# Latent attention's rotary part in one product: queries repacked two heads to a tile by moves within SBUF, and unread products in TensorE's pauses before two norms

## What is computed

```python
def rms_norm(x, g):
    y = xf * lax.rsqrt(jnp.mean(xf * xf, axis=-1, keepdims=True) + EPS)
    return y * g
...
hn = rms_norm(h, g_mix_pre); proj = hn @ w_in              # first block opens
...
h = h + rms_norm(merged @ w_out, g_mix_post)
hn = rms_norm(h, g_ffn_pre); f_gate, f_up = split(hn @ w_ffn_in)
...
q = (rms_norm_2(c_q, q_norm_g) @ w_uq)                     # 8 heads of 128 + 64
q_nope, q_rope = split(q, [128]); q_rope = rotary(q_rope)
k_nope, v = split(rms_norm_2(c_kv, kv_norm_g) @ w_ukv)
k_rope = rotary(k_rope)                                    # 64, shared by all heads
s = q_nope . k_nope + q_rope . k_rope                      # per head, 256 x 256
p = softmax(s * scale); o = p @ v
```

## Time and profile before

| | us |
|---|---|
| median of 3 executions | 2379.6 (2379.14 to 2380.88) |
| the profiled execution | 2379.67 |
| its span, first to last instruction | 2377.9 |
| TensorE busy | 2141.1 (90%) |
| VectorE busy | 1195.1 (50%) |
| ScalarE busy | 685.8 (29%) |
| GpSimd busy | 627.0 (26%) |

### The profile page before, as it was taken

One profiled execution on the slowest core, in us unless ns is written; L12 is line 12 of the kernel. 1 busy time (PEld: TensorE's weight loads), 2 busy tenths in 40 slices (PEclk: granted clock), 3 DMA queues, 4 the chain that ended last, 5 costly groups with the idle time before them and its releaser, 6 DMA issues.

```text
span 2377.9 us, 23241 instructions
## 1 busy us (share of the span) xinstructions
PE 2141.1 (90%) x7018; PEld 1291.6 (54%) x7018; DVE 1195.1 (50%) x2884; ACT 685.8 (29%) x1487; POOL 627.0 (26%) x545
## 2 busy tenths in 40 slices
PE   7999998999999999999897788889989998878786
PEld 6868886888885855444442222248644443322222
DVE  2982112000141035666666666633466666666664
ACT  1112101110110122343444343433243434343442
POOL 0210000000000001444454444410044555444442
PEclk9999998999999999999999999999999999999999
DMA  5443342444354325999999999983399999999997
GB/s 216 146 159 137 139 157 90 150 150 145 138 214 144 139 106 220 421 422 421 421 422 421 422 422 422 422 353 120 142 422 421 422 422 421 422 421 422 422 422 319
DMA packets 97560, 702.55 MB, mean 295 GB/s; under 512 B 10960, under 2 KB 11216, under 8 KB 12240
## 3 DMA queue, kind: packets, MB, share of 16 engines
q0 software_dynamic: 73728, 536.90, 54.3%
q1 hardware_dynamic: 21024, 149.96, 17.4%
q10 hardware_dynamic: 2736, 14.74, 1.6%
HBM read 700.51 MB, written 1.05 MB: 295 GB/s over the span
## 4 chain that ended last, share of the span: by engine, by line
PE 56%; DMA 30%; ACT 5%; issue 5%; DVE 3%; POOL 1%; DVEq 0%; POOLq 0%; ACTq 0%
DMA arena<-uv,expert_index 30%; PE acc L428 30%; PE aux L765 12%; PE acc L456 4%; PE aux L619 3%; PE acc L687 2%; PE acc L775 1%; ACT arena L1186 1%; ACT arena L1189 1%; ACT L1186 1%; PE aux L498 1%; ACT L1178 1%; DVE arena L1743 1%; POOL arena L963 1%; DVE arena L1380 1%
## 5 line engine op out<-in xcount | busy, mean ns | idle before, releaser
L765 PE MATMUL aux<-arena 128*128 128x512 f32 x2048 | 1007.7, 621 | 187.1 <-ACT arena L1189 182.3
L963 POOL DMA_INDIRECT arena<-uv,expert_index x512 | 601.4, 1175 | 1079.4 <-PE aux L765 606.6
L1743 DVE SCALAR_TENSOR_TENSOR arena<-arena 128x1024 f32<-128x1024 f32 x512 | 633.2, 1237 | 427.3 <-DMA arena<-uv,expert_index 426.5
L765 PEld LDWEIGHTS aux<-arena 128*128 128x128 f32 x2048 | 366.9, 193 | 728.2 <-ACT arena L1189 439.3
L428 PE MATMUL acc<-x,w_ring 128*128 128x256 f32 x2352 | 518.5, 384 | 14.6 <-DVE x L1344 9.3
L428 PEld LDWEIGHTS acc<-x,w_ring 128*128 128x128 f32 x2352 | 452.6, 193 | 79.9 <-issue 8.7
L1186 ACT ACTIVATE arena<-ident,dots 128x128 f32<-128x128 f32 x512 | 205.3, 401 | 704.6 <-DVE arena L1743 703.0
L428 PE MATMUL acc<-arena,w_ring 128*128 128x256 f32 x1032 | 225.0, 379 | 3.7 <-DVE arena L1440 1.6
L428 PEld LDWEIGHTS acc<-arena,w_ring 128*128 128x128 f32 x1032 | 195.7, 190 | 31.7 <-issue 2.6
L1189 ACT ACTIVATE arena<-arena,gate 128x128 f32<-128x128 f32 x512 | 205.4, 401 | 17.0
L949 POOL IOTA arena<- 128x512 int32 x1 | 0.6, 558 | 542.7 <-DVEq L1492 542.7
(11 more groups left out here) (250 smaller groups left out, 1169.9 us busy)
## 6 DMA issues: line engine op xcount, KB each, us to landing
w_ring<-stream SPq DMA_DIRECT2D x141, 1024.0 KB, 4.8
arena<-uv,expert_index POOLq DMA_INDIRECT x512, 14.9
first_query_weights<-first_heads ACTq DMA_DIRECT2D x4, 1024.0 KB, 14.3
row_vectors<-rows ACTq DMA_DIRECT2D x3, 1024.0 KB, 12.4
scratch<-keys ACTq DMA_DIRECT2D x2, 1024.0 KB, 6.2
x<-first_heads ACTq DMA_DIRECT2D x2, 1024.0 KB, 4.7
x<-x_cm SPq DMA_DIRECT2D x1, 1024.0 KB, 5.5
arena<-rows ACTq DMA_DIRECT2D x1, 1024.0 KB, 4.5
```

What stands on the lines that cost most here:

```text
L765: last = nc.tensor.matmul(AUX[2 * tt + c][:, :], DG[:, slot, :], G[:, slot, D + c * 512:D + (c + 1) * 512], start=False, stop=closes)
L963: pool.indirect_dma_start(G[:, s % RING, :], None, uv, bass.IndirectOffsetOnAxis(ap=EIDX[:, par, s:s + 1], axis=0),).then_inc(gathered[s % ...
L1743: v.scalar_tensor_tensor(G[:, slot, 0:D], G[:, slot, 0:D], 1.0, HTM[:, tt, :], ALU.mult, ALU.mult, accum_out=HD[:, slot:slot + 1]).then_in ...
```

## The change

It has three parts.

- **The rotary part.** The weight columns of the rotary key are laid out so that one tile `KR` holds the halves in the order first, second, first, second; the mask `half` (64 partitions each) makes two tiles `KRM` of it, for the even and the odd heads. The queries are rotated into `QR` as before, and then moved by eight transfers within SBUF into four tiles `QP`, each with both halves of two heads. Four of them (the even heads) are issued by GpSimd between the gathers of the two layers, four (the odd heads) by ScalarE after the second key copy; both wait for the rotation (`rotated`), and TensorE waits for the moves ahead of the first score. A score is then two products, plain and rotary.
- **Unread products.** Ten products of ones with ones, 128 x 128, into a bank that nobody reads then, ahead of the sums and again behind them, in the first norm and in the norm before the feed-forward.
- **The first norm.** x is loaded in four transfers, two issued by SyncE and two by ScalarE ahead of its other loads, and squared in four instructions, one for each.

TensorE at the program's start, before, and now. L498 and L502 are the sums, L428, L456, L432 and L460 projections, L535 is the unread product.

The diff, with little of its context:

```diff
@@ -70,7 +70,7 @@
          ("kv_norm", 2), ("ffn_g0", 8), ("ffn_b0", 8), ("freq_ret", 1),
-         ("freq_mla", 1), ("quarter", 4)]
+         ("freq_mla", 1), ("sign", 1), ("half", 2)]
 COL, _n = {}, 0
@@ -250,7 +250,7 @@
         CN = region(7, 5)
-        KR = region(12, 2)
+        KR = region(12, 1)
         QN = region(14, 12)
@@ -258,7 +258,8 @@
         OM = region(56, MLA_HEADS)
-        KRM = region(86, 8)
+        KRM = region(86, 2)
+        QP = region(88, 4)
@@ -313,7 +314,8 @@
         act_chain, dve_chain, pool_chain = sem("act_chain"), sem("dve_chain"), sem("pool_chain")
-        x_loaded, cols_loaded, rows_loaded = sem("x_loaded"), sem("cols_loaded"), sem("rows_loaded")
+        x_loaded = [sem(f"x_loaded{i}") for i in range(4)]
+        cols_loaded, rows_loaded = sem("cols_loaded"), sem("rows_loaded")
         small_loaded, sgu_w_loaded, pos_loaded = sem("small_loaded"), sem("sgu_w_loaded"), sem("pos_loaded")
@@ -345,6 +347,7 @@
         keys_loaded = sem("keys_loaded")
+        rotated, packed_even, packed_odd = sem("rotated"), sem("packed_even"), sem("packed_odd")
         head_scored = sem("head_scored")
@@ -360,7 +363,8 @@
         def _(sp):
-            sp.dma_start(X0[:, :, :], x_cm).then_inc(x_loaded, 16)
+            for j in (0, 2):
+                sp.dma_start(X0[:, 2 * j:2 * j + 2, :], x_cm[:, 2 * j:2 * j + 2, :]).then_inc(x_loaded[j], 16)
@@ -525,8 +529,15 @@
+            def idle_products(count):
+                for _ in range(count):
+                    nc.tensor.matmul(AUX[0][:, 0:P], ONES[:, :], ONES[:, :], start=True, stop=True)
             pe.wait_ge(ones_ready, 1)
-            square_sums()
+            idle_products(10)
+            square_sums(per=2)
+            idle_products(10)
@@ -841,7 +854,8 @@
             token_major(CN[:, 3:5, :], 2, 2)
-            need_input()
+            pe.wait_ge(packed_even, 16 * 4)
+            pe.wait_ge(packed_odd, 16 * 4)
             stored_by_evacuation(8)
@@ -850,8 +864,7 @@
                     nc.tensor.matmul(o, QN[:, e, qt * P:(qt + 1) * P], KN[:, e, :], start=True, stop=False)
-                    nc.tensor.matmul(o, QR[:, e // 4, qt * P:(qt + 1) * P], KRM[:, e % 4, :], start=False, stop=False)
-                    last = nc.tensor.matmul(o, QR[:, 2 + e // 4, qt * P:(qt + 1) * P], KRM[:, 4 + e % 4, :],
+                    last = nc.tensor.matmul(o, QP[:, e // 2, qt * P:(qt + 1) * P], KRM[:, e % 2, :],
                                             start=False, stop=True)
@@ -948,7 +961,18 @@
+            def pack(q):
+                for j in range(2):
+                    at = q % 2 * 64 + j * 32
+                    nc.gpsimd.dma_start(QP[at:at + 32, q // 2:4:2, :], QR[q * 32:q * 32 + 32, 2 * j:2 * j + 2, :])\
+                      .then_inc(packed_even, 16)
             for layer in range(2):
+                if layer:
+                    pool.wait_ge(rotated, 1)
+                    for q in (0, 2):
+                        pack(q)
                 uv = (uv0, uv1)[layer]
@@ -972,6 +996,8 @@
             n = dict(centred=0, scaled=0, roots=0)
+            for j in (1, 3):
+                act.dma_start(X0[:, 2 * j:2 * j + 2, :], x_cm[:, 2 * j:2 * j + 2, :]).then_inc(x_loaded[j], 16)
             act.dma_start(CO[:, :], cols).then_inc(cols_loaded, 16)
@@ -1013,8 +1039,10 @@
-            act.wait_ge(x_loaded, 16)
-            nc.scalar.activation(SC[:, :, :], X0[:, :, :], ACT.Square).then_inc(squares_ready, 1)
+            for j in range(4):
+                act.wait_ge(x_loaded[j], 16)
+                nc.scalar.activation(SC[:, 2 * j:2 * j + 2, :], X0[:, 2 * j:2 * j + 2, :], ACT.Square)\
+                  .then_inc(squares_ready, 1)
             root(RS)
@@ -1284,6 +1312,13 @@
                 evacuate(ACT.Copy, KN[:, 2 * s:2 * s + 2, :])
+                if s == 1:
+                    act.wait_ge(rotated, 1)
+                    for q in (1, 3):
+                        for j in range(2):
+                            at = 64 + j * 32
+                            act.dma_start(QP[at:at + 32, q // 2:4:2, :], QR[q * 32:q * 32 + 32, 2 * j:2 * j + 2, :])\
+                               .then_inc(packed_odd, 16)
             for c in range(2):
@@ -1360,7 +1395,8 @@
             dve.wait_ge(cols_loaded, 16)
-            dve.wait_ge(x_loaded, 16)
+            for j in range(4):
+                dve.wait_ge(x_loaded[j], 16)
             rstd(0, D, EPS)
@@ -1861,17 +1897,18 @@
-            rotate_mla(KR, (0, 1), CC[:, 5:7, :])
-            for r in range(2):
-                for q in range(4):
-                    v.tensor_scalar(KRM[:, 4 * r + q, :], KR[:, r, :], col("quarter", q), None, ALU.mult)
+            v.tensor_tensor(RA[:, 0, :], CC[:, 5, :], COS[:, 1, :], ALU.mult)
+            link(v.tensor_tensor(RB[:, 0, :], CC[:, 6, :], SIN[:, 1, :], ALU.mult))
+            link(v.scalar_tensor_tensor(KR[:, 0, :], RB[:, 0, :], col("sign"), RA[:, 0, :], ALU.mult, ALU.add))
+            for q in range(2):
+                v.tensor_scalar(KRM[:, q, :], KR[:, 0, :], col("half", q), None, ALU.mult)
             uq = ring.n
...
                 rotate_mla(QR, (half, 2 + half), QN[:, 8 + half:11 + half:2, :])
-            dve.sem_inc(input_ready, 1)
+            dve.sem_inc(rotated, 1)
@@ -1939,7 +1976,8 @@
     r1, r2 = m[:, 640:672], m[:, 672:704]
-    m = np.concatenate([m[:, :640]] + [r1] * 4 + [r2] * 4, axis=1)
+    m = np.concatenate([m[:, :640]] + [r1, r2] * 2 + [r2, r1] * 2, axis=1)
     t += _tiles(m, _cm((0, 1, 2, 5, 3, 4, 6), 8))
@@ -1980,7 +2018,8 @@
         "freq_ret": freqs(RET_DK)[:, None], "freq_mla": np.tile(freqs(64), 4)[:, None],
-        "quarter": (np.arange(P)[:, None] // 32 == np.arange(4)[None, :]).astype(np.float32),
+        "sign": np.where(np.arange(P) % 64 < 32, -1.0, 1.0).astype(np.float32)[:, None],
+        "half": (np.arange(P)[:, None] // 64 == np.arange(2)[None, :]).astype(np.float32),
     }
```

## The result

| | before | after |
|---|---|---|
| median of 4 executions, us | 2380.03 (2379.14 to 2380.88) | 2364.4 (2362.17 to 2367.18) |
| the profiled execution, us | 2379.67 | 2362.48 |

The ratio is 0.9934, with a 95% interval of 0.9918 to 0.995: 15.6 us less where 12.4 were forecast (2367.2).

What follows compares the result with a forecast made beforehand. A sequence of stages with different limits, TensorE holding 56% of the chain and bounding the attention; 6.2 (attention) + 4.7 (start) + 1.5 (second norm) = 12.4 us off 2379.6, so 2367.2 us, range 2362.5 to 2373.

Steps and rivals of the forecast that it cites:

- The attention, 6.2 us: Attention: two products fewer per head give 6.9 us, less waits, net 6.2 us; bounds 5.5 and 6.9.
- the wait of head 2: Attention: head 2 waits about 0.45 us for head 0's exponentials to free bank 0; gone from head 3 on.
- the wait of the first value products: Attention: the first value product waits perhaps 0.25 us for ScalarE's copy of the turned probabilities.
- Rival 2: Attention: ScalarE's and VectorE's chain binds every head, leaving 3.95 us there and 2369.5 us in all; chance 0.08.
- The moves, nothing: Repacking before the attention: the moves have 9.6 us before the first score, land by 1640 to 1643.5, and cost nothing.
- the slack that the prediction had named: Before the attention: TensorE reaches the third token-major bank at 1640.9, after ScalarE has caught up at 1638.6.
- The start, 4.7 us: Program start: 3.7 us from earlier, warmer sums plus 1.0 us of clock; bounds 1.9 and 6.2.
- nearer warm: First norm: sums end at 10.0 if warm or 12.3 if cold; 10.5 taken, against 14.20 before.
- the 1.0 us of clock from the second ten: Behind the first sums: the pause shrinks from 4.57 to 2.4 us and 1.0 of 1.96 us of half-clock loss returns.
- The second norm, 1.5 us: Norm before the feed-forward: 1.15 us from sums and up to 2.35 from clock; 1.5 taken, bounds 0 and 3.5.
- Remaining pauses of 2.5 to 2.9 us are over half of the old, so I take less than half: Second norm: the pauses left open by ten products decide the share of the bound of 3.5 us, so 1.5 taken.
- none of 2.4: Start: the rows show clock falls after pauses of 4.57, 5.05 and 4.74 us and none of 2.4 us.

Runs made afterwards that it cites:

- e3_idle: The kernel before with only the four groups of ten unread products added; 2374.21 us, ratio 0.9977.
- e6_start_groups: The changed kernel without the two groups of unread products at the second norm, those at the start kept; 2369.15 us, ratio 0.9954.
- e5_filled: The changed kernel with unread products filling long pauses: 19, 22 and 20 for three of the tens, new groups of 10, 11 and 13; 2360.57 us.
- e1_attention: The kernel before with only the rotary part (two products a query tile, repacking moves); 2373.18 us, ratio 0.9973.
- e2_split: The kernel before with only x loaded in four transfers and squared in four steps, no unread products; 2377.97 us, ratio 0.9991.
- e4_no_idle: The changed kernel without its four groups of unread products; 2371.91 us, ratio 0.9967.
- e7_norm_groups: The changed kernel without the two groups of unread products at the start, those at the second norm kept; 2368.59 us, ratio 0.995.
- e11_two_open: The kernel of `e10_unbroken` without its groups of 10 and 11 unread products at the pauses of 2.47 and 2.65 us; 2359.73 us, ratio 0.9923.
- e10_unbroken: The kernel of `e5_filled` with 12 instead of 10 unread products ahead of the first sums; 2359.33 us, ratio 0.9917.

## Why the prediction was right, and where it was not

**The attention, 6.2 us: 6.14 measured**, in two kernels. The wait of head 2 was 0.32 us (0.45 forecast), the spacing 3.03 (3.02), and the wait of the first value products about 0.1 us (0.25). TensorE stayed the bound, so two products a head were worth their time. Rival 2 (the chain of ScalarE and VectorE) didn't come.

**The moves, nothing: right with wrong prices.** ScalarE's issue took 0.67 us, not 0.46, and GpSimd's 0.56, not 1.24; the first error made ScalarE's two key copies 0.8 us later than forecast, the second had GpSimd done sooner; all moves had landed by about 1630 us. The error that mattered was absorbed by the slack that the prediction had named: four issues are hidden, and eight are not. The forecast of 2 to 3 us for a move of 64 KB was good (2.5 us for GpSimd's, 2.8 for ScalarE's). By "DMA: Bandwidth & Descriptors" (Trainium skill, Anatomy of one DMA), whose fit is for transfers that GpSimd issues, one of GpSimd's would take 2.15 us, as an estimate; the trace is 0.35 us above it, and it is the measured one that counts.

**The start, 4.7 us: 4.03 in one profile, 2.30 in the other.** The step "nearer warm" held in the first, where the sums (6.44 and 3.72 us) end at 10.16 against the 10.5 taken; in the second they were cold and the projection 1.7 us later. The step that failed is the 1.0 us of clock from the second ten. With the pause down to 2.33 us the first projections still fell to half clock, in both profiles and in those of `e3_idle` and `e6_start_groups` too, and they took 29.59 us as before, so the second ten gave nothing back. Two sizes under these steps were off as well. The fall costs 1.68 us (29.59 against 27.91 at full clock), not 1.96. The 1.96 came from the rate of the sums at 186.69, which is a little faster than that of the projections (and 29.59 less 27.6 is 1.99). And the warm sums took 3.72 us at the start, not 3.45. Only where the pause was filled down to 0.32 us did the clock stay up, in `e5_filled` and every kernel built on it.

**The second norm, 1.5 us: 3.3 in one profile, 1.1 in the other.** The failing step is "Remaining pauses of 2.5 to 2.9 us are over half of the old, so I take less than half". A pause's length doesn't give its price in proportion: behind it half clock comes or doesn't. Behind 2.33 us at the start it came each time, behind 2.42 us at the norm it didn't in the first profile, and did in the second. "TensorE: Matmul & The Clock Gate" (Trainium skill, What's actually happening) says that the moment of the change depends on where in a free-running count of the chip the activity falls, and varies from run to run. The two profiles of one kernel, with 3.72 and 5.35 us for the same sums, agree.

**What the forecast lacked: 3.5 us at two pauses that it never looked at.** The forecast has no term for a place without an edit, and where it looked for falls ("none of 2.4") it went by the edited places only. The trace of before has both of these falls, behind 2.47 and 2.65 us. In part it is luck, then, that the total came so near: in the first profile the start gave 0.7 us less than forecast, the norm 1.8 more, and these pauses 3.5 that weren't in the sum.

In six profiles (before, `e1_attention`, `e2_split`, `e4_no_idle`, `e6_start_groups`, `e7_norm_groups`) half clock set in 1.1 to 1.4 us after TensorE resumed from the first of them (at 635 to 640 us), each time; in the three with all four groups of ten (the changed kernel twice, `e3_idle`) it never did, and not in `e11_two_open`'s either. What tells them apart is when TensorE resumed after the last half-clock stretch ahead of it had ended: 241.0, 241.0, 240.9, 241.0 and 241.1 us in the first five, whose last such stretch was at the feed-forward's beginning (613.3 in the sixth, where it was at the start); 250.9, 240.4 and 250.7 in those that didn't. So my reading is that the clock changes on a beat of its own, and that a half-clock stretch, which slows the program until it ends, sets the program to that beat. The five with 241 us have a stretch of 6.8 us over the sums of the second norm and another over the feed-forward's beginning; they meet this pause at the same place of the beat every time, and lose every time. That there is half clock at the norm doesn't decide it alone: the second profile of the changed kernel had two stretches there as well, each half as long as theirs, resumed 240.4 us after the last and lost nothing. The scatter of `e11_two_open`, in which nothing sets the program, fits the reading. That is argued from rows, not shown: no run here moved the program by a known fraction of a microsecond, and the cause of the 3.5 us stays open to that extent.

**What is open.** Half clock followed a pause of 3.10 us near 1586 us (1576 after) in every profile that left it empty, all nine. Its price is 1.69 us by the rows of `e5_filled` above, but no run filled it alone, and why 3.10 us fell each time and 2.47 us didn't is not shown. The two slower executions of `e11_two_open` have no profile.

## What to carry to other kernels

An issue of a move costs time of the engine that issues it (0.67 us on ScalarE, 0.56 on GpSimd). Give moves to the engine that has nothing queued behind them, and cost them by what stands behind: eight on ScalarE cost 1.5 to 1.7 us, eight on GpSimd nothing. Where TensorE is the bound and pauses of 2.3 us and more lie in its path, fill them to the end with unread products. Four groups of ten, which leave 2.3 to 2.8 us of three of the four pauses open, were worth 7.5 us and scattered over 5. The four filled to the end, and three more pauses with them, were worth 12.1 (`e4_no_idle` lies 8.15 us below its "before", `e10_unbroken` 20.22 below its own) and scattered over 1.5. Before the time of such an edit is forecast, list every pause of similar length in the program, and not only the edited ones, since removing one half-clock stretch changes what the later pauses cost.

## What the hardware showed that was not expected

- Half clock can follow a pause of 2.33 to 2.65 us, and doesn't always: the same pause of 2.47 us was followed by a loss of 1.69 us in one kernel and by none in another.
- Ahead of the first change the granted clock reads 1.00 though the records are of half-clock length: in `e5_filled` it is 1.00 over sums that take 5.52 us where 3.72 is their time at full clock. At a program's start the records' durations tell the rate, not the clock column:

```profile
6.50:12.02 5.52, 5.52 (x16) 4.53 (x17) 0.00 (x0) 2.79 (x4) 0.00 (x0) 1.00 1.02 425
```

- GpSimd issues a plain move in 0.56 us, less than ScalarE's 0.67, though a gather costs it 0.94 and 0.30 more.
